# Layer-norm units and the last head's taps, placed by half pairs in the gate-b and branch stages of a decoder kernel

## What is computed

```python
proj = h @ w_mix_in[l]                    # q, k, v, u, gates
o = diff_attention(q, k, v, lam, rel_bias)           # 8 heads
o = rms_norm(o, subln_gain[l]) * (1 - lam_init)
y_attn = o.reshape(B, S, ATTN_W) @ w_attn_branch[l]
z = a * sigmoid(g)                        # a, g = split(u)
z = depthwise_conv(z, w_dw, width 31) + b_dw
z = silu(layer_norm(z, ln_g, ln_b))       # over the 1024 channels
y_conv = z @ w_conv_branch
merged = sigmoid(ga) * y_attn + sigmoid(gb) * y_conv
x = x + g2 * (merged @ w_mix_out[l])
```

## Time and profile before

| | us |
|---|---|
| median of 3 runs | 2736.06 |
| lowest and highest | 2736.03, 2737.34 |
| the profiled execution, its own time | 2737.03 |
| span of its trace | 2735.4 |
| PE busy | 2580.4 (94%) |
| DVE busy | 1708.0 (62%) |
| ACT busy | 1089.3 (40%) |

### The profile page before, as it was taken

One profiled execution on the slowest core, in us unless ns is written; L12 is line 12 of the kernel. 1 busy time (PEld: TensorE's weight loads), 2 busy tenths in 40 slices (PEclk: granted clock), 3 DMA queues, 4 the chain that ended last, 5 costly groups with the idle time before them and its releaser, 6 DMA issues.

```text
span 2735.4 us, 35015 instructions
## 1 busy us (share of the span) xinstructions
PE 2580.4 (94%) x11186; PEld 2035.2 (74%) x11186; DVE 1708.0 (62%) x2417; ACT 1089.3 (40%) x1561; POOL 81.4 (3%) x162
## 2 busy tenths in 40 slices
PE   4899998999999989999979999989999999899997
PEld 2688886777777768888868888867777778688886
DVE  3655567699997555543345556659999855655423
ACT  2443322555553434443234432245555443434422
POOL 0000010000000000000000001100000000000000
PEclk9999998999999999999989999999999999899998
DMA  6444464222222233543324446622222224343332
GB/s 223 142 146 139 150 225 154 74 84 74 83 85 77 86 113 116 154 126 93 97 82 148 147 133 211 215 66 81 77 84 78 75 85 130 101 146 101 97 97 89
DMA packets 472261, 320.38 MB, mean 117 GB/s; under 512 B 11303, under 2 KB 447785, under 8 KB 471176
## 3 DMA queue, kind: packets, MB, share of 16 engines
q1 hardware_dynamic: 445260, 227.69, 28.3%
q0 software_dynamic: 21888, 83.90, 9.1%
q10 hardware_dynamic: 5052, 8.02, 1.0%
HBM read 314.52 MB, written 5.05 MB: 117 GB/s over the span
## 4 chain that ended last, share of the span: by engine, by line
PE 70%; DVE 13%; issue 10%; ACT 4%; ACTq 1%; DVEq 1%
PE bank L1061 22%; PE bank L1063 21%; PE bank L1062 21%; DVE conv_part L868 5%; DVE rstd L626 3%; ACTq L419 1%; ACT w_hi L376 1%; PE bank L1079 1%; DVE w_lo L615 1%; PE bank L1080 1%; PE bank L1081 1%; DVE scaled L637 1%; PE bank L1116 1%; ACT probs L510 1%; ACT probs L517 1%
## 5 line engine op out<-in xcount | busy, mean ns | idle before, releaser
L615 DVE TENSOR_TENSOR w_lo<-w_raw,w_hi 128x1024 fp32r<-128x1024 f32 (+1 forms) x434 | 522.3, 1204 | 745.1 <-ACT w_hi L376 744.2
L1062 PE MATMUL bank<-h_lo,w_hi 128*128 128x512 f32 x2336 | 911.6, 390 | 0.0
L1061 PE MATMUL bank<-h_hi,w_hi 128*128 128x512 f32 x2208 | 885.6, 401 | 7.1 <-DVE w_lo L615 7.1
L1063 PE MATMUL bank<-h_hi,w_lo 128*128 128x512 f32 x2208 | 863.5, 391 | 0.0
L376 ACT ACTIVATE w_hi<-w_raw 128x1024 fp32r<-128x1024 f32 (+1 forms) x434 | 452.1, 1042 | 916.0 <-PE bank L1063 896.0
L1062 PEld LDWEIGHTS bank<-h_lo,w_hi 128*128 128x128 f32 x2336 | 440.4, 189 | 90.5 <-issue 3.8
L1061 PEld LDWEIGHTS bank<-h_hi,w_hi 128*128 128x128 f32 x2208 | 415.9, 188 | 119.4 <-issue 35.0
L1063 PEld LDWEIGHTS bank<-h_hi,w_lo 128*128 128x128 f32 x2208 | 415.7, 188 | 89.4
L868 DVE SCALAR_TENSOR_TENSOR conv_part<-glu,conv_taps,conv_part 128x512 f32<-128x512 f32 x464 | 317.5, 745 | 0.0
L1061 PE MATMUL bank<-s_hi,w_hi 128*128 128x512 f32 x704 | 274.9, 390 | 0.0
L1063 PE MATMUL bank<-s_hi,w_lo 128*128 128x512 f32 x704 | 274.0, 389 | 0.0
(11 more groups left out here) (157 smaller groups left out, 2333.4 us busy)
## 6 DMA issues: line engine op xcount, KB each, us to landing
w_raw<-in_ffn_w_in SPq DMA_DIRECT2D x176, 512.0 KB, 3.8
ada_raw<-in_ada_w POOLq DMA_DIRECT2D x144, 512.0 KB, 4.8
w_raw<-in_w_mix_in SPq DMA_DIRECT2D x112, 512.0 KB, 3.7
w_raw<-in_ffn_w_out SPq DMA_DIRECT2D x64, 512.0 KB, 3.7
w_raw<-in_ffn_w_out SPq DMA_DIRECT2D x32, 384.0 KB, 3.2
w_raw<-in_w_mix_out SPq DMA_DIRECT2D x18, 512.0 KB, 3.6
ada_first<-in_ada_w POOLq DMA_DIRECT2D x8, 1024.0 KB, 24.1
w_raw<-in_w_attn_branch SPq DMA_DIRECT2D x16, 512.0 KB, 3.7
```

Of the source, the lines that this page charges most:

```text
L615: dve.tensor_tensor(wlo[slot][:, 0:n, :], raw[slot][:, 0:n, :], whi[slot][:, 0:n, :].bitcast(F32), ALU.subtract).then_inc(w_lo[slot], 1)
L1061: pe.matmul(acc, wh, hi[:, k0 + k, :], start=first and k == 0, stop=False)
L1062: pe.matmul(acc, wh, lo[:, k0 + k, :], start=False, stop=False)
L1063: mm = pe.matmul(acc, wl, hi[:, k0 + k, :], start=False, stop=last and k == n - 1)
```

## The change

The table of units is keyed by round and half instead of by round, and starts a round later. On ACT and DVE a unit now stands behind its half's split instead of behind the round's second one. The last head's `unit_hi` moves from the end of round 0 to round 1 behind the first split. On DVE the head's `unit_gain` and `unit_lo` move to round 1, and the taps, which stood in rounds 0 and 1, go on to the second half of round 2. No operation is added or removed, and PE's own program is unchanged.

```diff
-LN_UNITS = {4: (0, 1), 5: (2, 3), 6: (4, 5, 6), 7: (7,)}
+LN_UNITS = {(5, 0): (0,), (5, 1): (1, 2), (6, 0): (3,), (6, 1): (4, 5), (7, 0): (6,), (7, 1): (7,)}
@@ ACT, round j
                     if j < KT // 2:
                         act.activation(GB[:, 2 * j, :], G[0][:, :], ACT.Tanh, scale=0.5).then_inc(acc_read[0], 1)
+                    if j == 1:
+                        unit_hi(l * UNITS + UNIT_HEAD + HEADS - 1, 0, AOHI[:, HEADS - 1, :])
+                    conv_units(j, 0)
...
-                    if j == 0:
-                        unit_hi(l * UNITS + UNIT_HEAD + HEADS - 1, 0, AOHI[:, HEADS - 1, :])
+                    conv_units(j, 1)
@@ DVE, round j, half t, behind w_lo_part (and gate_a from round 4)
                         if j == 0 and t == 0:
                             taps(HEADS - 1, 0, 5)
+                        if j == 0 and t == 1:
+                            taps(HEADS - 1, 5, 9)
+                            reciprocal(l * AUXN + AUX_HEAD + HEADS - 1, l * RSN + RS_HEAD + HEADS - 1)
                         if j == 1 and t == 0:
-                            taps(HEADS - 1, 13, 22)
-                    if j == 0:
-                        uh = l * UNITS + UNIT_HEAD + HEADS - 1
-                        reciprocal(l * AUXN + AUX_HEAD + HEADS - 1, l * RSN + RS_HEAD + HEADS - 1)
-                        unit_gain(uh, 0, True, OT[:, :], subg[:, ds(l, 1)])
-                        taps(HEADS - 1, 5, 8)
-                        unit_lo(uh, 0, AOLO[:, HEADS - 1, :], AOHI[:, HEADS - 1, :])
-                        taps(HEADS - 1, 8, 13)
-                    if j == 1:
-                        taps(HEADS - 1, 22, DVE_TAPS)
-                        chains(HEADS - 1)
+                            unit_gain(uh, 0, True, OT[:, :], subg[:, ds(l, 1)])
+                            taps(HEADS - 1, 9, 14)
+                        if j == 1 and t == 1:
+                            unit_lo(uh, 0, AOLO[:, HEADS - 1, :], AOHI[:, HEADS - 1, :])
+                            taps(HEADS - 1, 14, 20)
+                        if j == 2 and t == 0:
+                            taps(HEADS - 1, 20, 26)
+                        if j == 2 and t == 1:
+                            taps(HEADS - 1, 26, DVE_TAPS)
+                            chains(HEADS - 1)
+                        units = LN_UNITS.get((j, t), ())
+                        for n in units:
+                            unit_scale(ul + n, n % 2, n == 0, C[:, n, :])
+                        for n in units:
+                            unit_rest(ul + n, n % 2, CLO[:, n, :], CHI[:, n, :])
```

More of the change, by code:

```diff
@@ L558, in _, with conv_units @@
                     mix(h, False)
+                def conv_units(j, t):
+                    for n in LN_UNITS.get((j, t), ()):
+                        unit_split(l * UNITS + UNIT_LN + n, n % 2, n == 0, CHI[:, n, :], ACT.Silu,
+                                   PT[:, ds(l * PC + PC_LNG + n, 1)], PT[:, ds(l * PC + PC_LNB + n, 1)])
                 for j in range(KT):
@@ L587, in _ @@
                         root(l * AUXN + AUX_VAR, l * UNITS + UNIT_LN)
-                    for n in LN_UNITS.get(j, ()):
-                        unit_split(l * UNITS + UNIT_LN + n, n % 2, n == 0, CHI[:, n, :], ACT.Silu,
-                                   PT[:, ds(l * PC + PC_LNG + n, 1)], PT[:, ds(l * PC + PC_LNB + n, 1)])
                 with act.Fori(0, KT // 2) as i:
@@ L968, in _ @@
                 dve.wait_ge(acc_read[1], l * USES + USE0["gb"])
+                uh, ul = l * UNITS + UNIT_HEAD + HEADS - 1, l * UNITS + UNIT_LN
                 for j in range(KT):
@@ L1006, in _ @@
                         reciprocal(l * AUXN + AUX_VAR, l * RSN + RS_VAR)
[L1007 to L1014, removed]
                 with dve.Fori(0, KT // 2) as i:
```

## The result

The changed kernel takes **2743.82 us** (median of 11 runs, 2741.51 to 2745.37) against 2736.06 us for the kernel before (11 runs, 2734.55 to 2739.53). The ratio is 1.0027, with a 95% interval of [1.0018, 1.0036]: slower by about 7.8 us, with 4.9 and 9.9 us as the ends. The forecast was 2743.5.

What follows compares the result with a forecast made beforehand. PE, busy 94% of the span, was taken as the bound. 2 x (2.28 + 2.4 - 2.6 + 1.6) = +7.4 us on the profiled 2737.03, less 1.0 to the median, gave 2743.5 us; range 2738.5 to 2748.

Steps and rivals of the forecast that it cites:

- The long waits ahead of pairs 2 and 6 go: PE's waits in gate-b and the branch stage, 3.53 and 3.13 us in layer 1, would be gone.
- The sum ends 2.28 us later and PE waits 9.4 us: Gate-b: two more splits of 1.14 us ahead of DVE's channel sum delay it; PE waits at the mean.
- part 1: Taps and last head's norm reordered in gate-b: +4.7 us a layer at the variance mean, 2.28 plus 2.4.
- ACT and DVE set the pace in the branch stage: From 892 on, halves take 5.13 us with one unit, 6.56 with two, against PE's 5.45; gain 2.6 a layer.
- The clock falls behind the wait at unit 7, 1.6 us: Branch stage: a new PE wait of 2.7 to 3.0 us lowers the clock, costing 1.6 us a layer, ends 0 and 2.9.
- The clock behind the mean, 2.4 us: Gate-b: half clock behind PE's 9.4 us wait, 5.2 us at 0.46 each, costs 2.4 a layer, between 1.6 and 2.9.
- units keep up with PE: Rival, branch stage: PE meets no wait from pair 6 on, gaining 6.5 instead of 2.6 us; 2732.5 us; chance 0.04.
- The wait at unit 7 leaves the clock up: Rival, branch stage: no low clock there; 2741.9 us if in one layer, 2740.3 in both; chance 0.33.
- Unit starts cost more: Rival, branch stage: six starts each wait 0.29 us more for `scaled`, losing 1.5 us a layer; 2746.5 us; chance 0.13.
- The sum is not later: Rival, gate-b: something other than `running_sum` holds PE's mean, so reordering taps costs little or nothing; 2734 us; chance 0.05.
- the third case: In the list of chances, unit starts in the branch stage cost more: 0.13, entered as 0.12 in the slower sum.

Runs made afterwards that it cites:

- PE kept busy: The changed kernel with 40 more unused 128x512 matmuls in each layer ahead of PE's wait for the channel sum; 2740.04 us, ratio 1.0013.
- taps alone: The kernel before with only the taps and the last head's norm laid out by half pairs, units unchanged; 2743.04 us, ratio 1.0023.
- early sum: The changed kernel with the last eleven taps and the channel sum put back ahead of both splits of pair 3; 2741.32 us, ratio 1.0009.
- the fastest one here: The kernel before with units by half pairs in another lay-out, 0 and 1 starting in round 5's first half; 2723.14 us, ratio 0.9948.

## Why the prediction was right

Step by step, by its own numbers:

- *The long waits ahead of pairs 2 and 6 go*: they did, in both layers.
- *The sum ends 2.28 us later and PE waits 9.4 us*: from the split of (1, 1) to PE's mean 27.21 before, 29.40 after, 2.19 more; the wait is 9.41. The experiment with the sum ahead of pair 3's splits showed that it is those two splits. From the mean to the variance mean part 1 then added 1.16 and 1.25, so it cost 3.3 and 3.5 us a layer where 4.7 was forecast.
- *ACT and DVE set the pace in the branch stage*. Behind the variance mean, forecast and measured: high part of (6, 1) 13.1 and 13.06; (7, 0) 19.6 and 19.59; (7, 1) 24.7 and 24.69; (8, 0) 31.3 and 31.20; (8, 1) 36.4 and 36.30; PE's restart 42.4 to 42.7 and 42.55. The rows behind three of them:

```profile
896.28 1.05 ACT L376 ACTIVATE w_hi<-w_raw 128x1024 fp32r<-128x1024 f32 x1
...
914.42 1.04 ACT L376 ACTIVATE w_hi<-w_raw 128x1024 fp32r<-128x1024 f32 x1
...
919.52 1.04 ACT L376 ACTIVATE w_hi<-w_raw 128x1024 fp32r<-128x1024 f32 x1
```

- *The clock falls behind the wait at unit 7, 1.6 us*: it did in both layers of the profile (0.76 over 7 us, as in the earlier trace rows behind the wait of 3.13). The price is 132.66 less the 131.04 of layer 1 with PE kept busy, where it did not fall: 1.62.
- *The clock behind the mean, 2.4 us*: **the term that was mis-sized** for this profile. The stretch took 1.16 and 1.25 more than in the kernel before. Part of the price is hidden in that, since 0.26 came back at PE's start on pair 3, where the prediction said that nothing comes back; against the kernel with PE kept busy the price is 1.42 and 1.54. That too lies below the low end given, 1.6. The clock had come back 3 us after the mean's start, as the stretches ahead of and behind 859 show:

```profile
852.00:859.00 7.00, 0.00 (x0) 0.00 (x0) 6.76 (x10) 0.00 (x0) 0.00 (x0) 0.50 0.26 79
859.00:866.00 7.00, 6.96 (x23) 5.00 (x24) 3.80 (x7) 1.86 (x3) 0.00 (x0) 0.79 0.00 0
```

  0.79 over 7 us is 2.9 us at half. The eight stretches that the forecast went by were said to start at 3.5 us; the one behind 83.57 has 0.76 over 7 us, which is 3.4. In six further cases of a wait ahead of the mean (taps alone with 9.4 us, and both profiles of the early sum with 7.14) the stretch took 2.55, 1.57, 2.54, 2.32, 2.22 and 2.10 more than before, so all eight have a mean of 2.0: the size of the term was near, its low end was not low enough. The rate of 0.46 us for each at half gives 2.9 x 0.46 = 1.3 here. By the Trainium skill's TensorE: Matmul & The Clock Gate, section Terms, the estimate is 1.45; the 1.42 measured against the kernel with PE kept busy agrees with it.

The profiled layers add up to 5.0 us where the sum said 7.4, and the medians differ by 7.8. Not all of this agreement is merit. The profile fell on short low stretches, the runs spread over 3.9 us, and the interval of the ratio is 5 us wide. That the median came within 0.3 us of the forecast is luck; the mechanism is borne out far better than the last microsecond.

Of the rivals, *units keep up with PE* was false for this lay-out and was made true by another, at about the time that its working gave (tile 7 at 38.3 us behind the variance mean, 38.6 forecast). *The wait at unit 7 leaves the clock up* did not happen in the profile of the changed kernel, but it did in three of eight such waits of the other kernels, so in some of the eleven runs it may have. *Unit starts cost more* was a guess from one row: the four starts between the first and the last took 0.85 or 0.86 behind `scaled`, and only the last one 1.13 again. *The sum is not later* fell with the 2.19 us. One slip in the chances: the third case counts in all, so slower adds up to 0.65 and not 0.64.

## What to carry to other kernels

A long wait of the busiest engine is worth nothing if the next meeting point is set by another engine that has no gap: sum that engine's work up to the meeting point, and move work behind it, not ahead of it. When an engine works through a chain beside fixed slots, compare the chain's length per slot with the slot (5.1 and 6.5 against 5.45 here) and put the long pieces where a slot has room; the same idea at the right place gave 14 us. And count a stop of an engine that has no slack behind it twice, once as a wait and once for the clock that may fall behind it.

## What the runs showed of the hardware

Whether a wait of PE brings its clock down is not a property of the wait alone. Over all profiles here, in the gate-b and branch stages:

| wait of PE, us | followed by half clock, of cases |
|---|---|
| up to 1.8 | none |
| 2.98 to 3.03 (unit 7) | 7 of 10 |
| 3.12 to 3.17 (pair 6) | 3 of 4 |
| 3.41 and 3.45 | 1 of 2 |
| 3.53 to 3.56 (pair 2) | 6 of 6 |
| 7.14 and 9.4 (the mean) | 8 of 8 |

The stretch at half lasted from none to 6.0 us behind the same wait of the same kernel. That kernel's runs lie in two groups some 8 us apart, and in the profiles of the two its waits agree within 0.05 us while the stretches behind them do not; that this makes the groups is the likely reading and not shown run by run. The sum of the prediction took the fall behind the wait at unit 7 as full, with a chance of 0.45 for both layers; it happened in 7 of 10 cases. Whether a kernel without such waits is also steadier is not shown: the fastest one here had 2721.84 to 2724.28, but in 5 runs only, and it keeps the 3.56 us wait ahead of pair 2.
